# Opening of a transformer block in six groups of tiles instead of five, accumulators added on VectorE, column sums set among the products

## What is computed

```python
c_act = silu(c)
mod = c_act @ w_ada[l] + b_ada[l]              # 2048 -> 6 * 2048
shift1, scale1, gate1, shift2, scale2, gate2 = split(mod, 6)
h = rms_norm(x, norm1_w[l]) * (1.0 + scale1) + shift1
proj = h @ w_in[l]                             # then attention, gates, FFN
```

## Time and profile before

| what | value |
|---|---|
| median of 3 runs | 2665.84 us (2662.67 to 2668.75) |
| profiled execution, its own time | 2669.94 us |
| its span | 2668.4 us |
| TensorE busy | 2637.7 us (99%) |
| VectorE busy | 1987.0 us (74%) |
| ScalarE busy | 1057.3 us (40%) |
| mean granted TensorE clock | 0.993 |
| first unit's first product | 58.80 us |

### The profile page before, as it was taken

The page is one execution under the profiler, slowest core; times in us unless marked ns, Lnnn a source line. Parts: engine busy times, 40 slices in busy tenths (PEclk is TensorE's granted clock), DMA queues, the critical chain, the costliest instruction groups (busy, mean ns, idle before and its releaser), DMA issues.

```text
span 2668.4 us, 44554 instructions
## 1 busy us (share of the span) xinstructions
PE 2637.7 (99%) x17140; PEld 2407.3 (90%) x17140; DVE 1987.0 (74%) x3044; ACT 1057.3 (40%) x1437; POOL 309.5 (12%) x289
## 2 busy tenths in 40 slices
PE   7999999999999999999999999999999999999998
PEld 7877888888888888888899999999999999999998
DVE  6878888843333367765568888888888888888896
ACT  5343333433343332222344444444444444434443
POOL 0023333210000111223100000000000000010100
PEclk8899999999999999999999999999999999999999
DMA  9866667633333367777434444444444469495753
GB/s 360 301 181 202 183 187 205 181 95 102 96 102 95 105 203 236 246 229 227 150 95 158 159 148 149 159 148 149 158 148 149 158 217 339 159 356 180 263 213 119
DMA packets 387485, 487.71 MB, mean 183 GB/s; under 512 B 18932, under 2 KB 314120, under 8 KB 386792
## 3 DMA queue, kind: packets, MB, share of 16 engines
q1 hardware_dynamic: 348912, 352.47, 42.0%
q0 software_dynamic: 32752, 126.75, 13.5%
q10 hardware_dynamic: 5640, 5.89, 0.6%
HBM read 415.32 MB, written 69.73 MB: 182 GB/s over the span
## 4 chain that ended last, share of the span: by engine, by line
PE 93%; DVE 3%; DMA 1%; issue 1%; ACT 1%; SPq 0%; DVEq 0%; ACTq 0%
PE bank L989 15%; PE bank L992 15%; PE bank L991 15%; PE bank L656 12%; PE bank L658 12%; PE bank L657 12%; DVE ada_acc L1447 1%; PE bank L814 1%; DMA ramp_w<-in_w_ada 1%; PE bank L728 1%; PE bank L729 1%; PE bank L730 1%; PE bank L840 1%; PE bank L710 1%; PE bank L803 1%
## 5 line engine op out<-in xcount | busy, mean ns | idle before, releaser
L989 PE MATMUL bank<-mov,w_slot 128*128 128x256 f32 x3472 | 980.3, 282 | 0.8 <-ACT blocks L1338 0.8
L992 PE MATMUL bank<-mov,w_slot 128*128 128x256 f32 x3472 | 978.9, 282 | 0.0
L991 PE MATMUL bank<-mov,w_slot 128*128 128x256 f32 x3472 | 978.6, 282 | 0.0
L989 PEld LDWEIGHTS bank<-mov,w_slot 128*128 128x128 f32 x3472 | 661.7, 191 | 1.1 <-ACT blocks L1338 1.0
L991 PEld LDWEIGHTS bank<-mov,w_slot 128*128 128x128 f32 x3472 | 662.1, 191 | 0.0
L992 PEld LDWEIGHTS bank<-mov,w_slot 128*128 128x128 f32 x3472 | 661.6, 191 | 0.0
L656 PE MATMUL bank<-h_hi,w_hi 128*128 128x512 f32 x1248 | 493.6, 396 | 0.0
L658 PE MATMUL bank<-h_hi,w_lo 128*128 128x512 f32 x1248 | 487.5, 391 | 0.0
L657 PE MATMUL bank<-h_lo,w_hi 128*128 128x512 f32 x1248 | 486.7, 390 | 0.0
L1426 DVE TENSOR_TENSOR w_lo<-w_raw,w_hi 128x1024 fp32r<-128x1024 f32 x188 | 239.6, 1275 | 296.2 <-ACT w_hi L1019 295.8
L1277 ACT ACTIVATE w_slot<-w_raw 128x768 fp32r<-128x768 f32 x248 | 209.6, 845 | 541.8 <-PE bank L992 537.2
(11 more groups left out here) (268 smaller groups left out, 2949.4 us busy)
## 6 DMA issues: line engine op xcount, KB each, us to landing
w_raw<-in_w_ffn_in SPq DMA_DIRECT2D x352, 256.0 KB, 3.1
w_raw<-in_w_ada SPq DMA_DIRECT2D x128, 512.0 KB
w_raw<-in_w_ffn_out SPq DMA_DIRECT2D x88, 512.0 KB, 5.7
u_fm<-u_stage POOLq DMA_DIRECT2D x22, 1792.0 KB, 8.4
mov<-u_fm POOLq DMA_DIRECT2D x22, 1792.0 KB, 21.9
w_raw<-in_w_in SPq DMA_DIRECT2D x128, 256.0 KB
w_raw<-in_w_in SPq DMA_DIRECT2D x60, 512.0 KB
ramp_w<-in_w_ada SPq DMA_DIRECT2D x24, 1024.0 KB, 12.9
```

Source lines behind the costliest of these rows:

```text
L989: nc.tensor.matmul(dst, lhsT=wh, rhs=xh, start=s == 0 and t == 0, stop=False, skip_group_check=True)
L991: nc.tensor.matmul(dst, lhsT=wh, rhs=xl, start=False, stop=False, skip_group_check=True)
L992: mm = nc.tensor.matmul(dst, lhsT=wl, rhs=xh, start=False, stop=last, skip_group_check=True)
```

## The change

The groups become 2, 4, 4, 2, 2, 2 tiles. After a group's 16 accumulations VectorE adds the odd accumulator to the even one (`ramp_summed`), so that one matmul for each column is left. The column matmuls of groups 1 to 5 stand singly among the products of units 1, 5, 7, 11 and 13 (`COLS_AMONG`), one behind each product, the first of them behind a wait for the addition; those of group 0 alternate with fills. ScalarE copies the sums out of PSUM into `ada_sum` in one instruction (`cols_out`) and reads them there. Fills stand ahead of units 0, 1, 2, 5, 6 and 14, behind a wait for the last copy. Accumulators, places of h_low, first_low and weight loads are set anew.

```diff
-RG = (4, 4, 4, 2, 2)
-RG0 = (0, 4, 8, 12, 14)
+RG = (2, 4, 4, 2, 2, 2)
+RG0 = (0, 2, 6, 10, 12, 14)
...
-        ramp_acc = [(at("ramp_even0", TAB, 2 * S), at("ramp_odd0", WORK, 2 * S)),
-                    (at("ramp_even1", STORE, 2 * S), at("ramp_odd1", FORGET, 2 * S)),
...
+        ramp_acc = [(at("ramp_even0", TAB, S), at("ramp_odd0", TAB + T, S)),
+                    (at("ramp_even1", FORGET, 2 * S), at("ramp_odd1", WORK, 2 * S)),
+                    (at("ramp_even2", TAB, 2 * S), at("ramp_odd2", STORE, 2 * S)),
...
-        COLS_BEHIND = {2: 1, 6: 2, 9: 3, 12: 4}
-        FILL = (18, 6, 5, 0, 0)
+        COLS_AMONG = {1: 1, 5: 2, 7: 3, 11: 4, 13: 5}
+        FILL = {0: 8, 1: 22, 2: 4, 5: 8, 6: 3, 14: 5}
...
-            first_behind = {2: 0, 5: 1, 6: 2, 8: 3, 9: 4, 12: 5, 13: 6, 16: 7}
+            first_behind = {2: 0, 7: 1, 8: 2, 10: 3, 12: 4, 14: 5, 17: 6, 20: 7}
...
-            def ramp_cols(p):
-
+            def begin_cols(p):
                 if p:
-                    pe.wait_ge(ramp_mod, RG0[p] // GK)
-                fill(4, FILL[p])
-                pe.wait_ge(ada_mac, macs_to(STEP * p + STEP - 1))
-                for t in range(2 * RG[p]):
-                    for n in range(2):
-                        mm = nc.tensor.matmul(bank[4][:, t:t + 1], lhsT=ramp_acc[p][n][:, t * P:(t + 1) * P],
-                                              rhs=ones[:, 0:1], start=n == 0, stop=n == 1)
-                mm.then_inc(ada_cols, RG[p])
+                    pe.wait_ge(cols_out, p)
+                pe.wait_ge(ramp_summed, p + 1)
+
+            def ramp_col(p, t):
+
+                mm = nc.tensor.matmul(bank[4][:, t:t + 1], lhsT=ramp_acc[p][0][:, t * P:(t + 1) * P],
+                                      rhs=ones[:, 0:1], start=True, stop=True)
+                if t == 2 * RG[p] - 1:
+                    mm.then_inc(ada_cols, RG[p])
...
+                among, columns = COLS_AMONG.get(k), 0
...
+                    for w, x in ((wh, xh), (wh, xl), (wl, xh)):
+                        mm = nc.tensor.matmul(dst, lhsT=w, rhs=x, start=k == 0 and w is wh and x is xh,
+                                              stop=k == KD - 1 and w is wl)
+                        if among is not None and columns < 2 * RG[among]:
+                            if columns == 0:
+                                begin_cols(among)
+                            ramp_col(among, columns)
+                            columns += 1
...
-            ramp_cols(0)
+            begin_cols(0)
+            for t in range(2 * RG[0]):
+                fill(4, 1)
+                ramp_col(0, t)
             pe.wait_ge(xn_copied, KD)
-            fill(7, 8)
             pe.wait_ge(fl_ready, 1)
             for k in range(KD):
+                if k in FILL:
+                    pe.wait_ge(cols_out, 1 + sum(behind < k for behind in COLS_AMONG))
+                    fill(4, FILL[k])
                 first_unit(k)
...
+                nc.scalar.activation(ada_sum[:, 0:2 * n_k], bank[4][:, 0:2 * n_k], ACT.Copy).then_inc(cols_out, 1)
+                act.wait_ge(cols_out, p + 1)
...
-                            mod_op = nc.scalar.activation(mod[:, n:n + 1], bank[4][:, c:c + 1], ACT.Identity,
+                            mod_op = nc.scalar.activation(mod[:, n:n + 1], ada_sum[:, c:c + 1], ACT.Identity,
...
-                    if p == 1:
+                    if p == 2:
                         dve.wait_ge(xn_ready, KD)
                     if p >= 2:
-                        dve.wait_ge(ramp_mod, RG0[p - 1] // GK)
+                        dve.wait_ge(ramp_mod, (1, 3, 3, 5)[p - 2])
...
-            h_behind = {(1, 4): 0, (1, 5): 1, (1, 7): 2, (1, 8): 3, (2, 5): 4, (2, 6): 5, (2, 8): 6, (2, 9): 7,
-                        (3, 9): 8, (3, 11): 9, (3, 13): 10, (3, 15): 11, (4, 11): 12, (4, 13): 13}
-            w_behind = {(1, 1): 0, (1, 6): 1, (1, 12): 2, (2, 7): 3, (2, 12): 4, (3, 12): 5, (4, 1): 6, (4, 14): 7}
+            h_behind = {(1, 7): 0, (1, 8): 1, (2, 5): 2, (2, 6): 3, (2, 8): 4, (2, 9): 5, (3, 10): 6, (3, 12): 7,
+                        (3, 14): 8, (3, 15): 9, (4, 10): 10, (4, 12): 11, (5, 11): 12, (5, 13): 13}
+            w_behind = {(1, 1): 0, (1, 12): 1, (2, 7): 2, (2, 12): 3, (3, 13): 4, (4, 2): 5, (4, 14): 6, (5, 14): 7}
...
+                dve.wait_ge(ada_mac, macs_to(STEP * p + STEP - 1))
+                v.tensor_tensor(ramp_acc[p][0][:], ramp_acc[p][0][:], ramp_acc[p][1][:], ALU.add).then_inc(ramp_summed, 1)
```

More of the change, by code:

```diff
@@ L241, in build_block @@
         ada_acc = at("ada_acc", WORK, 4 * UN)
-        ramp_acc = [(at("ramp_even0", TAB, 2 * S), at("ramp_odd0", WORK, 2 * S)),
-                    (at("ramp_even1", STORE, 2 * S), at("ramp_odd1", FORGET, 2 * S)),
-                    (at("ramp_even2", TAB, 2 * S), at("ramp_odd2", WORK, 2 * S)),
-                    (at("ramp_even3", FORGET, S), at("ramp_odd3", FORGET + T, S)),
-                    (at("ramp_even4", TAB, S), at("ramp_odd4", TAB + T, S))]
+        ramp_acc = [(at("ramp_even0", TAB, S), at("ramp_odd0", TAB + T, S)),
+                    (at("ramp_even1", FORGET, 2 * S), at("ramp_odd1", WORK, 2 * S)),
+                    (at("ramp_even2", TAB, 2 * S), at("ramp_odd2", STORE, 2 * S)),
+                    (at("ramp_even3", WORK, S), at("ramp_odd3", WORK + T, S)),
+                    (at("ramp_even4", FORGET, S), at("ramp_odd4", FORGET + T, S)),
+                    (at("ramp_even5", TAB, S), at("ramp_odd5", TAB + T, S))]
         ada_acc2 = at("ada_acc2", FORGET, 4 * UN)
@@ L295, in build_block @@
             sem("x_turned"), sem("xt_copied"), sem("xt_dve"), sem("x_spilled"), sem("xn_ready"), sem("xn_copied"))
+        ramp_summed, cols_out = sem("ramp_summed"), sem("cols_out")
         gate_done, gate_out, gate_early = sem("gate_done"), sem("gate_out"), sem("gate_early")
@@ L727, in first_unit @@
                         wh, wl, dst = whi[:, cols], wlo[:, cols], bank[b][:]
-                    nc.tensor.matmul(dst, lhsT=wh, rhs=xh, start=k == 0, stop=False)
-                    nc.tensor.matmul(dst, lhsT=wh, rhs=xl, start=False, stop=False)
-                    mm = nc.tensor.matmul(dst, lhsT=wl, rhs=xh, start=False, stop=k == KD - 1)
+                    for w, x in ((wh, xh), (wh, xl), (wl, xh)):
[6 more added lines that the diff above has]
+                            columns += 1
                     if k == KD - 1 and t == 5:
@@ L744, in _ @@
                 normalised(k)
-            ramp_cols(0)
+            begin_cols(0)
+            for t in range(2 * RG[0]):
+                fill(4, 1)
+                ramp_col(0, t)
             pe.wait_ge(xn_copied, KD)
-            fill(7, 8)
             pe.wait_ge(fl_ready, 1)
             for k in range(KD):
+                if k in FILL:
+                    pe.wait_ge(cols_out, 1 + sum(behind < k for behind in COLS_AMONG))
+                    fill(4, FILL[k])
                 first_unit(k)
-                if k in COLS_BEHIND:
-                    ramp_cols(COLS_BEHIND[k])
             def y_post(y, evicted):
```

## The result

The changed kernel takes 2674.48 us (median of 10 runs, 2671.63 to 2675.63) against 2665.73 us (10 runs) before: a ratio of 1.0031, 95% interval 1.0023 to 1.004. It is 8.75 us slower. The forecast was no change (2666.0, range 2659 to 2674); the range missed the median by half a microsecond. The rival that came nearest is the third, the clock, at +8; it is right in part only, as the part on the forecast says.

The account below looks back on a forecast made before the run. TensorE, busy for 2637.7 of 2668.4 us, was taken as the bound. Earlier start and new waits left the opening at 157.5 against 157.4: +0.1 us on 2669.94, which stands 4.1 above the median, so 2666, range 2659 to 2674.

Parts of the forecast that it names:

- the third, the clock: Rival, the same as (c): clock falls in the opening bring +8 us, 2674; chance 0.21.
- What the change takes off TensorE: Opening: 28 column matmuls for 48, 42 fills for 11; 100.3 us from first product, no shorter in itself.
- Unit 0: First unit starts at 47.7 instead of 58.8 us, after 4 us idle on TensorE; a clock fall expected.
- The 22 fills behind unit 0 absorb that: Behind unit 0: the fills take up the clock fall expected after TensorE's idle 4 us.
- Unit 7: First real wait, for group 3's addition: 4 us, plus 1 us for the clock (bounds 0 and 2.5).
- The tail: Behind unit 9: unit 12 starts 12.6 us later after a 2 us wait; stage ends 35.1 us behind unit 9.
- The sum: Opening stage ends at 157.5 against 157.4 us before, +0.1 us; bounds 153.8 and 160.7.
- (b): Waits at units 7 and 12 don't come, as chunks land sooner: -8.5 us, 2657, half gives 2661; chance 0.22.
- (c): Clock falls at units 5, 7 and 13, 3 us each: +8, 2674; with two of them +5; chance 0.21.
- Short chunks: Opening's loads: short chunks at 359 GB/s against 382 for long ones; 8.4 MB take 1.4 us longer.
- The estimate of 2.6 us: Loads: at the skill's 341 GB/s for 1 MB, the same 8.4 MB would take 2.6 us longer.

Follow-up runs that it names:

- fills_fewer: Changed kernel with 15 fills instead of 22 ahead of unit 1; 2671.6 us, 1.0027 of before.
- fills_front: Changed kernel with 17 fills instead of 8 ahead of unit 0; 2676.1 us, 1.0041 of before.
- fills_unit7: Changed kernel with 7 fills added ahead of unit 7; 2671.1 us, 1.0021 of before.
- sums_unit8: Changed kernel with the sums of group 3 in unit 8 instead of unit 7; 2667.1 us, 1.0008 of before.
- moves_fills: Changed kernel, group 3's sums in unit 8, first_low 6 behind accumulation 5 of group 5, 17 fills ahead of unit 0, none ahead of 14; 2665.8 us.
- sums_in_run: Changed kernel with a group's column matmuls in one run behind the unit's first product instead of singly; 2672.4 us, 1.0027 of before.
- moves_both: Changed kernel with group 3's sums in unit 8 and first_low 6 behind accumulation 5 of group 5; 2668.4 us, 1.0012 of before.
- before_added: Kernel before with only VectorE's addition of the accumulators and one column matmul instead of two; 2662.3 us, 0.9988 of before.

## Where the forecast held and where it failed

That the change is worth little held: 0.3% of the kernel. Its point and its range did not. The walk by engines named the waits in their places; three terms of the sum and its base were mis-sized. From the walk to the first profile the opening ends 6.8 us late: 3.1 us ahead of unit 7, 2.0 us from there to the end of unit 9 (2.4 more for the clock, 0.7 less for the wait, 0.3 not placed), 1.7 us in the tail.

- **What the change takes off TensorE**: right. TensorE's busy time did not change.
- **Unit 0**: starts at 49.26, forecast 47.7. Chunk 5 didn't set it, as I had said; VectorE's own order did (group 1 began at 37.49, held 0.4 us by first_high 0).
- **"The 22 fills behind unit 0 absorb that"**: this sentence failed. Fills are instructions with a length, not slack. Unit 0 ran at half clock until about 55, the fills then started at 56.85 instead of 52.5, and took their 9.5 us all the same. The sums of group 1 were over at 70.0 instead of 66.1, 3.9 us late, VectorE stood 2.10 us for h tile 2, and the addition of group 2 ended at 92.5 instead of 89.3. fills_fewer and fills_front show the link: both bring unit 9 some 3 us earlier. What it costs the kernel they don't show, as the time of neither is clearly better.
- **Unit 7**: a wait of 3.31 us (forecast 4), because TensorE was itself late. The low clock behind it had been put at 1 us with 2.5 as the upper bound; it lasted from about 109.6 to 116.5, half of which is 3.4 us, and fills_unit7 gives 3.2. The upper bound was too low, although group 1 had shown 3.2 us. This is the largest single term, and sums_unit8 shows the place to matter: 5.9 us in the time.
- **The tail**: unit 12 starts 12.9 us behind unit 9, forecast 12.6; what set it was not chunk 22, as the sum had it (5.4 us and four accumulations, 8.05 in all), but VectorE's twelve accumulations, 8.0 us from the addition (131.53) to h_low 12 (139.56). That the two are equally long is luck; the last part was 36.8 us, forecast 35.1. Most of the 1.7 is a third fall of the clock, priced at nothing. In the second profile it didn't come, and the last part took 35.8.
- **The sum**: 157.5 forecast, 164.3 and 163.3 in two profiles. The base, 157.4, was 3.1 us above the second profile of before, whose execution stood at the median. I had noted that the first stood 4.1 us above the median and subtracted that from the total, as if it lay outside the opening; 3.1 of the 4.3 us by which the two spans differ lie in the stage that the change shortens.
- **The rivals**: (b) is out, as the additions of groups 3 and 4 came later than walked, not 3 us sooner. (c) came near in its number, +8 against 8.75, and that is in part luck: of the three falls that it names, at units 5, 7 and 13, only the one in unit 7 came. The others came at units 0 and 12, behind waits, and 3.1 us are the base. In the changed kernel the clock stayed up in unit 5, among the sums.
- **Short chunks**: slower, as the row said. From 24 to 30 us, where the changed kernel loads short chunks and the one before long ones, both with weights beside them, the four profiles have 360 and 359 GB/s against 383 and 385. VectorE went on with group 0's last chunk at 32.05, forecast near 31. The estimate of 2.6 us took the speed of 1 MB DMAs for them, but those are the long ones' (1024 KB each); the short ones' are 512 KB. Of group 3, the chain passes through a load of 5.91 us that lands at 100.95, the late end of what I had walked. What that costs by itself no run shows.

The two windows, of the changed kernel and of the one before:

```profile
24.00:30.00 6.00, 6.00 (x40) 6.00 (x39) 5.01 (x8) 2.81 (x5) 0.00 (x0) 0.69 1.09 360
24.00:30.00 6.00, 6.00 (x54) 6.00 (x54) 2.79 (x3) 3.67 (x7) 0.00 (x0) 0.96 1.05 383
```

Shown by runs, over before of the same set: the place of group 3's sums, 5.9 us, and all places and fills together, 8.1 us (moves_fills), both clear of noise. Shown by profiles, with times that point the same way but don't settle it: the low clock behind the wait in unit 7 (3.2 us), first_low 6 (2.2 to 3.2 us), the fixed fills (3 us at unit 9, and 1.9 at the end for those ahead of unit 14). They overlap and don't add up. Only argued: that one chunk load and VectorE are the bound of the mended kernel. Not tried: other group sizes with the additions, and ScalarE's copy out of PSUM by itself.

## What to carry to other kernels

A fill helps where it stands in the wait itself, ahead of the instruction that would wait (fills_unit7: clock 1.00 behind it, unit 9 over 3.7 us earlier); behind the wait it is fixed work that delays everything queued after it. Even in the wait it is no sure gain: fills_front kept the clock up in unit 0, and its time was no better. When an order is brought forward so that a consumer meets its producer, price each new wait twice, once for the wait and once for the clock behind it. Before a sum is made against one profile, look whether the time by which that execution stands off its median lies in the stage that is changed. And compare two variants through the runs of a common kernel in the same set, not by their medians: here that turned a gain of 2.9 us into one of 1.4.

## What the runs showed of the hardware

Whether the clock falls behind the same instructions differs between executions: behind the 3.8 us run of group 1's sums it fell in one profile of before and not in the other. Behind the wait of 2.30 us ahead of unit 12 it fell in two of six profiles (changed and sums_unit8, but not the second of changed, fills_fewer, fills_unit7 and sums_in_run), and the longer waits there of 3.36 us (moves_both) and 3.02 us (moves_fills) left it at 1.00, while 3.54 us (fills_front) did not. Eight narrow matmuls, in one run or spread over eight products, left it at 1.00 in the changed kernel and in sums_in_run; spread in the same way in moves_fills, and in one run behind a wait of 2.92 us in before_added, they did not. The Trainium skill ("TensorE: Matmul & The Clock Gate", Part 1) warns that the number of slow matmuls varies from run to run; these profiles agree.

Where loads of 512 KB stand in the place of loads of 1024 KB, from 24 to 30 us, 360 GB/s were moved instead of 383. Their rows in w_ada are half as long too (256 against 512 values), so the runs don't show which of the two does it.
